# A spectral convolution's last three result stores cut into channel halves, and the inverse transform's first jobs reshaped to fit

## What is computed

```python
y = jnp.fft.irfft(jnp.fft.rfft(s, n=n, axis=1) * jnp.fft.rfft(g, n=n, axis=0)[None],
                  n=n, axis=1)[:, :L]
y = (y + s * skip.astype(jnp.float32)).astype(u.dtype) * x0
return y @ w_out + b_out
```

## Time and profile before

| | |
|---|---|
| median of three runs | 2446.01 us (2444.39 to 2450.88) |
| profiled execution | 2445.98 us, its span 2444.2 us |
| TensorE busy | 2360.0 us, 97% of the span |
| VectorE, ScalarE, GpSimd busy | 1107.9, 604.0, 657.8 us |
| granted TensorE clock, mean | 0.986 |
| spectral part, inverse, first panel of wout | about 370 to 445, 454 to 495, 481 to 498 us of the span |

### The profile page before, as it was taken

How to read it: one execution, slowest core, us unless ns; L and a number is a source line. 1 busy time by engine, 2 the same in 40 slices (tenths; PEclk the granted TensorE clock), 3 DMA queues, 4 the chain that set the end, 5 groups by cost and what they waited for, 6 DMA issues and landing times.

```text
span 2444.2 us, 29269 instructions
## 1 busy us (share of the span) xinstructions
PE 2360.0 (97%) x11692; PEld 1899.7 (78%) x11692; DVE 1107.9 (45%) x1131; ACT 604.0 (25%) x672; POOL 657.8 (27%) x378
## 2 busy tenths in 40 slices
PE   7999999799999999999997999999999999999996
PEld 5666773478888888888886888889897877778885
DVE  6765445542662165413366837263543124500533
ACT  4333324422100001002123636262622011111011
POOL 2212211122333333323241121222222233323331
PEclk9999999999999999999998999999999999999998
DMA  4133239512221223112111212020214221112231
GB/s 155 51 122 123 85 134 369 187 43 78 95 86 52 77 80 109 43 43 70 51 61 35 104 36 69 26 77 26 77 34 181 94 78 56 56 43 69 95 121 69
DMA packets 77507, 211.51 MB, mean 87 GB/s; under 512 B 24182, under 2 KB 28088, under 8 KB 77178
## 3 DMA queue, kind: packets, MB, share of 16 engines
q1 hardware_dynamic: 64794, 172.72, 20.7%
q10 hardware_dynamic: 8288, 29.36, 3.1%
q0 software_dynamic: 4352, 8.40, 1.1%
HBM read 165.36 MB, written 40.37 MB: 84 GB/s over the span
## 4 chain that ended last, share of the span: by engine, by line
PE 75%; DVE 3%; ACT 1%; issue 0%; ACTq 0%; DVEq 0%
PE ps L1209 63%; PE ps L539 5%; DVE T L1857 1%; PE ps L1483 1%; PE ps L586 1%; PE ps L605 1%; PE ps L568 1%; PE ps L606 1%; PE ps L607 1%; PE ps L1231 0%; DVE XN L1887 0%; PE ps L1240 0%; DVE X L2181 0%; DVE H L1880 0%; PE ps L505 0%; PE ps L524 0%
## 5 line engine op out<-in xcount | busy, mean ns | idle before, releaser
L1209 PE MATMUL ps<-H,whi 128*128 128x512 f32 x4000 | 1082.3, 392 | 21.9 <-DVE H L1924 11.3
L1209 PEld LDWEIGHTS ps<-H,whi 128*128 128x128 f32 x4000 | 749.9, 188 | 198.5 <-issue 29.6
L1209 PE MATMUL ps<-H,wlo 128*128 128x512 f32 x2000 | 617.7, 390 | 0.0
L1156 POOL CAST whi<-wraw 128x1024 fp32r<-128x1024 f32 x174 | 182.5, 1049 | 1573.0 <-PE ps L1209 844.9
L1158 POOL TENSOR_TENSOR wlo<-wraw,whi 128x1024 fp32r<-128x1024 f32 x178 | 453.6, 2548 | 53.4 <-ACT whi L673 39.5
L1209 PEld LDWEIGHTS ps<-H,wlo 128*128 128x128 f32 x2000 | 376.5, 188 | 79.3
L1209 PE MATMUL ps<-A,whi 128*128 128x512 f32 x1472 | 397.8, 392 | 8.2 <-DVE A L2213 4.9
L1209 PEld LDWEIGHTS ps<-A,whi 128*128 128x128 f32 x1472 | 278.0, 189 | 68.0 <-issue 5.3
L1209 PE MATMUL ps<-A,wlo 128*128 128x512 f32 x736 | 228.1, 391 | 0.0
L1209 PEld LDWEIGHTS ps<-A,wlo 128*128 128x128 f32 x736 | 139.3, 189 | 29.3
L2097 DVE TENSOR_TENSOR T<-ps,T 128x1024 f32<-128x1024 f32 x22 | 26.9, 1224 | 155.7 <-PE ps L1209 155.7
(11 more groups left out here) (337 smaller groups left out, 2310.6 us busy)
## 6 DMA issues: line engine op xcount, KB each, us to landing
wraw<-in_panels SPq DMA_DIRECT2D x181, 512.0 KB, 3.6
mw<-in_modp SPq DMA_DIRECT2D x24, 512.0 KB, 3.5
g<-gsp SPq DMA_DIRECT2D x16, 512.0 KB, 3.7
gr<-g SPq DMA_DIRECT2D x16, 512.0 KB, 9.8
bs<-s SPq DMA_DIRECT2D x16, 512.0 KB, 9.4
YB<-yi POOLq DMA_DIRECT2D x16, 512.0 KB, 8.8
X<-in_xT SPq DMA_DIRECT2D x4, 1024.0 KB, 10.8
s<-sa SPq DMA_DIRECT2D x8, 512.0 KB, 2.7
```

The costliest lines, as they stand in the source:

```text
L1156: nc.gpsimd.tensor_copy(whi[:, s, :, :], wraw[:, s, :, :]).then_inc(hi_made, 1)
L1209: last = mm(p[:, c * step:(c + 1) * step], w[:, ws, k, :], operand(act, a, k, c * step, step), start=(q == 0 and w is whi and a == 0), sto ...
```

## The change

The stores of groups 13, 14 and 15 are cut by channels: channels 0 to 511 first, counted by `y_stored(g)` as before, and channels 512 to 1023 counted by a new semaphore `y_late`. GpSimd issues the first half of 13, the first half of 14, the second half of 13, the first half of 15, and the second halves of 14 and 15. TensorE waits for the first halves before the inverse, and for all three second halves before each rows job whose channels begin at 512 or above. SP waits for the second halves too before it issues the first panels of `wout`, and GpSimd before it splits them. The first two jobs of INV take 128 channels and all 16 residues each (16 products of 128 columns instead of 8 of 256), so that tile 0 can follow the first and tile 1 the second; the new order is rows, rows, tile 0, rows, tile 1, rows, rows, tile 2, rows, tile 3, and on as before. One of the semaphores for loads of the spectral part is shared with an older one, to make room for `y_late`.

```diff
-INV = [("rows", 0, 256, 8 * _m) for _m in range(2)]
-for _c in range(1, 4):
+INV = [("rows", 0, 128, 0), ("rows", 128, 128, 0), ("tile", 0), ("rows", 256, 256, 0), ("tile", 1), ("rows", 256, 256, 8)]
+for _c in range(2, 4):
     for _m in range(2):
         INV.append(("rows", 256 * _c, 256, 8 * _m))
         INV.append(("tile", 2 * _c - 2 + _m))
@@
-        gr_in = [(sem(f"gr_in{u}"), 0) for u in range(3)]
+        gr_in = [(filt_in, 208), (sem("gr_in1"), 0), (sem("gr_in2"), 0)]
@@
+        y_late = sem("y_late")
+        Y_HALVES = range(GROUPS - 3, GROUPS)
@@
             sp.wait_ge(*y_stored(GROUPS - 2))
+            sp.wait_ge(y_late, 16 * len(Y_HALVES))
             panel(n, n % 2)
             panel(n + 1, (n + 1) % 2)
@@
             for g in range(GROUPS):
                 pool.wait_ge(spec_ev, g + 1)
-                pool.dma_start(YB[y_rows(g), :, :], yi[g % 3][:, :]).then_inc(y_stored(g)[0], 16)
-            for g in range(GROUPS - 3, GROUPS):
+                if g not in Y_HALVES:
+                    pool.dma_start(YB[y_rows(g), :, :], yi[g % 3][:, :]).then_inc(y_stored(g)[0], 16)
+                else:
+                    pool.dma_start(YB[y_rows(g), :, 0:T // 2], yi[g % 3][:, 0:T // 2]).then_inc(y_stored(g)[0], 16)
+                    for b in ((), (g - 1,), (g - 1, g))[g - Y_HALVES[0]]:
+                        pool.dma_start(YB[y_rows(b), :, T // 2:T], yi[b % 3][:, T // 2:T]).then_inc(y_late, 16)
+            pool.wait_ge(y_late, 16 * len(Y_HALVES))
+            for g in Y_HALVES:
                 pool.wait_ge(*y_stored(g))
@@
                 if kind == "rows":
                     c0, w, m0 = j
+                    if c0 >= T // 2:
+                        pe.wait_ge(y_late, 16 * len(Y_HALVES))
                     for u in range(T // w):
```

## The result

The changed kernel takes 2467.84 us (median of five runs, 2463.84 to 2472.84), the kernel before in the same comparison 2447.55 (2444.39 to 2450.88). The ratio is 1.0084, with 95% from 1.0071 to 1.0097: slower by 20 us, where 2442.3 was forecast. The profiled execution took 2464.41 us, its span 2462.6, 18.4 more than before. The prediction was wrong.

The account below looks back on a forecast made before the run. TensorE's panel products were taken to bound the kernel, so only its stops can give time. An earlier restart (-3.0 us) and the order (-0.7) made -3.7 from 2445.98: 2442.3 us, range 2438.8 to 2447.6.

Parts of the forecast that it names:

- what VectorE's chain gains, the span gains: Inverse stage: VectorE is later the bound, so time its chain of operations saves shortens the whole run equally.
- The landing: Before the inverse: group 15's first half lands 5.0 us after issue instead of 8.0, worth -3.0 us.
- R': TensorE's forecast restart at the inverse after the change: 451.4 us, against R = 454.40 before.
- I put the 1.8 us between 6.2 and 8.0 down to this: Group 15's store takes longer than group 14's because panels and X move beside it; 1.8 us of contention goes.
- The rival of stores that go one by one: GpSimd's store queue needs some 4 us per transfer whatever its size: +2.4 us, 2448.4 us; chance 0.12.
- The order: Inverse stage: tile 0 moves ahead of one rows job, starting VectorE 1.9 us earlier; worth only 0.7 us.
- What is late next: Inverse stage: ScalarE's high part of tile 1 comes at R' + 19.0 to 19.2; VectorE waits about a microsecond.
- The covers: Panels and X move some 4 us later, with over 15 us of cover; second halves have 10: cost nothing.
- The pairs: First two rows jobs: 128-column products still pair on array halves, adding nothing; rival without pairing 2446.1 us, chance 0.09.
- The first stop: TensorE's wait before the inverse for group 15's store: near 6.6 us, not 9.6.
- The clock rival: After the restart the clock still returns at 460.2, so the gain is -2.2 us, 2443.8 us; chance 0.18.
- The second slow stretch: Rival: TensorE's half-clock stretch from 494.36 to 497.7 goes too: -5.4 us, 2440.6 us; chance 0.16.

Follow-up runs that it names:

- 68 instructions: Kernel before plus 68 idle instructions (long settled waits) on TensorE in its stop ahead of the inverse; 2467.42 us, ratio 1.008.
- quiet store: Kernel before, whole stores and old order, with SP also waiting for group 15's store before issuing the panels; 2446.64 us, ratio 0.9995.
- half by SP: Changed kernel's halves with the old list of jobs, group 15's first half issued by SP instead of GpSimd; 2444.4 us, ratio 0.9989.
- only group 15 cut: Kernel before with only group 15's store in halves, 13 and 14 whole, SP holding the panels back; 2445.33 us, ratio 0.9995.
- halves only: Changed kernel with the old list INV, so only the stores of groups 13 to 15 travel in halves; 2442.63 us, ratio 0.9973.
- after, 32 more: Changed kernel plus 32 idle instructions on TensorE ahead of the inverse, 100 more than before in all; 2443.53 us, ratio 0.9986.
- new jobs, whole stores: Kernel before with only the new list INV, whole stores, padded to 96 instructions more; 2447.8 us, ratio 0.9997.

## Why the prediction was wrong, step by step

**The step that failed** is the cost of the added instructions. "Calls double from 8 to 16 ... and I add nothing for both jobs together" asked whether the products themselves take longer. They don't. But 68 instructions more in TensorE's program were costed at nothing as instructions, in the one place that mattered, ahead of a loop whose code had 14 to 23 instructions of room before an eighth block. In their place the runs show 18.3 us: three stops of 5.9 us, the lower clock at them, and 2.2 us unassigned. With "what VectorE's chain gains, the span gains" the prediction then carried the seam's gain to the end as if the rest of the program were untouched. None of the rivals had a cost outside the seam. The profile of before shows that its code is loaded about once (q8, 53 packets for a program of 54.1 blocks), but not how many blocks a loop may touch, so none of its rows gives the price; that there was one to ask for, the prediction overlooked.

**The landing: the sum right, the terms not.** Forecast: 5.0 us to the landing of the half (1.2 saved by size, 1.8 by the absence of the panels), R' 3.0 us earlier. Measured in after:

```profile
DMA to landing us min/median/max: 4.1/4.5/4.5
```

Its own size gave 1.6, the cut of groups 13 and 14 gave 1.4, and the panels only 0.6: 8.0 - 3.6 = 4.4. The step "I put the 1.8 us between 6.2 and 8.0 down to this" failed. 1.2 of the 1.8 us between the stores of groups 14 and 15 are there without the panels; that they come of group 14's store, issued 3.1 us ahead, is argued from the 1.4 and not shown by itself. A term for the cut of the stores ahead was missing. That the sum came near all the same is luck. The rival of stores that go one by one, some 4 us each, falls: three transfers in the queue, and the half that counts is down after 4.5 us.

The Trainium skill (DMA: Bandwidth & Descriptors, section Rules for kernel authors) advises against two transfers to disjoint halves of the partitions, because they serialize. These are halves of the channels, so the rule doesn't speak of them; here a half that must be down first, with the rest behind it, brought TensorE's restart 3.5 us forward. The Trainium skill's formula (the same page, Anatomy of one DMA) would give, as an estimate, 3.2 us for 512 KB and 2.6 for 256 KB; the rows say 6.2 to 8.0 and 4.4 to 5.8.

**The order.** It must be read with the clock taken out, since the clock comes back at another distance from the restart in each kernel:

| kernel | order | restart | clock back after | restart to MEMSET | less half the slow stretch |
|---|---|---|---|---|---|
| before | old | 454.40 | 5.7 | 41.40 | 38.55 |
| 68 instructions | old | 452.33 | 3.9 | 40.58 | 38.6 |
| quiet store | old | 451.22 | 5.3 | 41.17 | 38.5 |
| half by SP | old | 450.73 | 3.9 | 40.52 | 38.6 |
| only group 15 cut | old | 453.33 | 2.7 | 39.92 | 38.6 |
| halves only | old | 450.51 | 2.6 | 40.47 | 39.2 |
| after | new | 451.98 | 5.3 | 40.39 | 37.7 |
| after, 32 more | new | 450.99 | 4.5 | 40.18 | 37.9 |
| new jobs, whole stores | new | 452.81 | 5.0 | 40.21 | 37.7 |

(Times in us, each from one execution; the clock by windows of 0.5 us.) The new order is worth 38.6 - 37.8 = 0.8 us; 0.7 was forecast. Up to tile 7 (487.20, 35.22 behind the restart instead of 36.23) it is 1.0 with the clock's share left in. The halves-only kernel stands 0.6 off its own group; the next point but one has the cause. The medians of the kernels with and without the order (2443.53 and 2442.63) can't tell 0.8 us.

**What is late next.** "The order is worth 0.7 and not 1.9; ScalarE's copy is what is late next" can be seen in the kernel with the new jobs and whole stores, whose VectorE waits for tile 1's high part:

```profile
471.45 1.22 DVE L2057 TENSOR_TENSOR A<-T,A 128x1024 fp32r<-128x1024 f32 x1 [0.77 <-ACT A L1650]
```

That is R' + 18.64 with a stop of 0.77; "19.0 to 19.2" and about a microsecond were forecast. In after the same operation runs at R' + 18.83, but with no stop, since VectorE has lost that time already:

```profile
460.72 1.97 DVE L2081 TENSOR_TENSOR T<-T,G 128x1024 f32<-128x1024 f32 x1
...
463.92 3.20 DVE L2081 TENSOR_TENSOR T<-T,G 128x1024 f32<-128x1024 f32 x1
```

```profile
459.25 2.35 POOL L1161 TENSOR_TENSOR wlo<-wraw,whi 128x1024 fp32r<-128x1024 f32 x1
461.54 2.04 POOL L1159 CAST whi<-wraw 128x1024 fp32r<-128x1024 f32 x1
463.66 2.38 POOL L1161 TENSOR_TENSOR wlo<-wraw,whi 128x1024 fp32r<-128x1024 f32 x1
```

**The covers.** They held for TensorE: panels 4.9 us later at 454.17, the first cast at 458.12 instead of 455.64, and no wait of TensorE for the second halves is in the trace. (It stands before the fifth rows job, not the sixth; the time given, R' + 12 us, is the fifth's.) One thing was overlooked. GpSimd's split of the panels used to be over before VectorE multiplied by the gate. Now it is moved back by 2.5 us and VectorE comes earlier, so the two meet, and the multiplication takes 1.97 and 3.20 us instead of 1.22 to 1.23. In the kernel with whole stores, where the second split ends at 460.9, both take 1.22 to 1.23. X was under way in that kernel too (issued at 449.31, down after 16.6 us), so it isn't X that slows them. These 2.7 us fall into the time in which VectorE would have waited for ScalarE and cost nothing in after (37.7 as with whole stores). In the halves-only kernel the second multiplication took 3.16 beside the same split, and VectorE goes straight from it to tile 0's low part, at R' + 15.14; less half the slow stretch that is 13.8, where before and the kernel with the half by SP, both with a wait for ScalarE there, have 13.2. These are its 0.6 us.

**The pairs** held: two jobs of 3.76 us and half of 5.3 us at the lower clock make 6.4, the row says 6.26. The first stop was forecast at 6.6 us and measured at 6.11. **The clock rival** put its return at the same point of time; it came 5.3 us behind the restart in after, at 457.3 us of the span and not 460.2, and 2.6 to 5.7 in the others. Two kernels with whole stores and the old order have 3.9 and 5.3, so no part of this is the change's for certain. **The second slow stretch** stayed: 487.9 to 494.8 after, 490.9 to 497.7 before.

Without the loop's stops, then, the whole came out near the forecast: 2443.53 us for the changed kernel with 32 idle instructions, 2442.63 for the halves alone, against 2442.3. The kernel before took 2448.18 beside them, and the forecast had started from 2445.98, so the gains are 4.7 and 5.6 us, where 3.7 and, for the halves alone, 3.0 were forecast.

## What to carry to other kernels

Before adding instructions to an engine that has an on-chip loop further on, count where the loop begins and ends in blocks of its code, and read the instruction queue's packets and the waits "issue" at the loop's turns: a change can be right where it is made and lose elsewhere. If a change costs time that its place doesn't show, pad it with idle instructions and see whether the time goes. Where one DMA is waited for, try cutting it and those ahead of it in its queue, so that what is needed first is small and goes first; here the cut of the ones ahead was worth nearly as much (1.4 us) as its own (1.6).

## What the runs showed of the hardware that I hadn't expected

- TensorE ran a loop of 1591 instructions without fetching it anew while it touched seven blocks of 256, and fetched 27 packets of 16 KB more over its three turns when it touched eight.
- The refetching cost nothing where the loop began 45 to 54 instructions ahead of a block's end, and about 2 us a turn where 1 to 10 were left. At three stops, 5.9 us in all, the clock was at 1.2 GHz for 20.4 us, which by half of it cost more (10.2) than the stops. With 25 to 34 left, a stop of 0.55 us had 3.4 us of it and one of 0.66 us none.
- The store of 512 KB to eight partitions took 7.4 us with nothing in its way but the one ahead of it; 256 KB behind such a whole store took 5.8, and behind two halves that go to different partitions 4.4; the issuing queue didn't matter.
- VectorE's multiplication of 128x1024 took 3.20 us instead of 1.23 while GpSimd worked on tiles of the same size, and GpSimd's cast took 2.04 instead of 1.03.
- Ahead of the inverse, 324 instructions of long settled waits held TensorE for 35.66 us, 0.11 each; behind the loop 68 of them didn't lengthen a stop of 4.87 us.
